# First head group of a hybrid mLSTM/SSD decoder layer: the order of its projection units, and the engine that evacuates the values

## Chip, cores and metric

One core of one Trainium2 chip. The metric is the device time of one execution in microseconds (us), the median of three runs.

## What is computed

The reference is a trunk of two layers (D_MODEL 1024, SEQ 256, everything float32). Each layer runs a SwiGLU feed-forward half step, the mixer, a second feed-forward half step and a gated per-layer input. The change lies in the mixer:

```python
u = rmsnorm(h, g_mix[i])
proj = u @ w_in[i]
q, k, v, o_pre, i_pre, f_pre, z, xbc, dt_raw, gate_pre = jnp.split(proj, split_at, axis=-1)
ha = mlstm_chunkwise(q, k, v, i_pre + b_igate[i], f_pre + b_fgate[i])
ha = rmsnorm(ha, g_mlstm_head[i]) * jax.nn.sigmoid(o_pre)
xbc = jax.nn.silu(causal_dwconv(xbc, conv_w[i], conv_b[i]))
xs, bm, cm = jnp.split(xbc, ...)
dt = jax.nn.softplus(dt_raw + dt_bias[i])
yb = ssd_chunked(xs, dt, -jnp.exp(a_log[i]), bm, cm)
yb = rmsnorm((yb + xs * d_skip[i]) * jax.nn.silu(z), g_ssm_out[i])
merged = sigmoid(g_a) * (ha @ w_branch_a[i]) + sigmoid(g_b) * (yb @ w_branch_b[i])
h = h + merged @ w_out[i]
```

There are four head groups. The 256 tokens are two chunks of 128.

## The kernel before, in words

**Units.** All weights go through in units of 1 MB (8 blocks of 128 rows by 256 columns) in a ring of three slots. For each unit the SyncE queue loads the raw weights (`load`, L285 to L290), ScalarE rounds them to a high part (`hi`, L518), VectorE subtracts to get the low part (`lo`, L823), and TensorE multiplies high by high, high by low and low by high. A feature-major unit (`feat`, L1377) is 48 matmuls over all 256 tokens; the values' unit (`tok`, L1389 to L1391) has the tokens as its output rows, chunk 0 first and then chunk 1. `unit_done` counts finished units, and `hi` of a slot waits for the unit that used the slot before.

**A head group** has nine units, in this order: BC (B and C), QK, X01, X23, V, Z0, Z1, O, GA. Unit number p writes PSUM bank p modulo 3, and VectorE evacuates it (`evac`, L1034; V at L1118; QK at L1104 and L1106). `evac` is one semaphore that counts these evacuations in order. `unit` on TensorE waits for the low part of its weights and for the evacuation that frees its bank.

**Each engine has its order written out by hand** in `groups`, with one body for the first group and one for the other three, which run in a loop. `step(p)` on ScalarE and on VectorE is `hi` and `lo` of unit p + 2. So the order of the steps among the other operations sets when weights are ready.

**The norm ahead of the first group.** `features` (L540, ScalarE) evacuates the transposed activations of a chunk to `u_hi`; `low` (L866, VectorE) makes `u_lo`; `mean_square` (L549) the sums of squares. For the mixer (n == 1) VectorE does both chunks' residuals (L872) first and then both chunks' `low`. Units are not scaled by the norm on their way in; `rms` is applied in the evacuation: `row_scale` makes a diagonal (`rdiag`, L853, VectorE), TensorE spreads it over partitions (`norm_rows`, L1431), ScalarE copies it to `rB` (L569).

**Once per layer, inside the first group:** TensorE multiplies the 40 columns of gates and dt (`small`, L1522); VectorE scales the rows (`pre_row`, L1097); TensorE turns them back (`small_back`, L1528); VectorE computes softplus and `dA` (`softplus_gates`, L950 to L982; the exponential at L653 and `e_a` at L655 are ScalarE's); TensorE transposes (`gates`, L1535 to L1539); VectorE scans the gate rows (`gate_rows`, L989 to L1012), TensorE turns them to columns (`gates_back`, L1545), ScalarE writes `tokc` (L671, L672).

**Per group:** a causal convolution of four taps on three pairs of tiles (`conv`, L1045 and L1048, VectorE), each followed by a tanh on ScalarE (`tanh_conv`, L625) and a product on VectorE (`silu`, L1059). GpSimd builds `R` (L424), from which TensorE makes the decays (`segments`, L1563; `from_start`, L1569) and ScalarE their exponentials (`decay`, L630; L638). GpSimd multiplies them by the masked scores (L464, L468) and the mLSTM weights by a mask (L458). VectorE clips distances (L1075), weighs scores (L1087), masks (L1081) and weights the inputs (L1125, L1129). TensorE does `scores` (L1584), `cb` (L1577), `chunk_heads` (L1592), the transposes of the inputs (L1602), `memory_read` (L1608), `state` (L1614) and `outputs` (L1625, L1627). The head norm (L1169 to L1189) ends in transposes (L1686). In the loop body `from_start` stands in the middle of the V unit, and it waits for `decay(1)`, which ScalarE does behind the tanh of the second convolution.

Of the kernel before, what the change touches and what calls it, by code (L numbers as in the profile page):

```python
# [12 lines left out]
P = 128  # L13
# [10 lines left out]
def trunk(nc, T, out):  # L24
# [36 lines left out]
    BC, QK, X01, X23, V, Z0, Z1, O, GA = range(GU)  # L61
    K_MIX = U_FFN
# [6 lines left out]
    NE = NG * GU + 4  # L69
# [4 lines left out]
    with ctx:  # L74
# [134 lines left out]
        r_i, a5 = at("r_i", [MH, S], F32, a5)  # L209
        r_f, a5 = at("r_f", [MH, S], F32, a5)  # L210
# [35 lines left out]
        names = """up0_done h1T_done res_done uT_done gate_done y_out_ready rB_ready z_tanh o_tanh gate_tanh evac par_ready rdiag_ready rB_done ydiag_ready yB_done yB_ready wsm_hi_ready wsm_ready pre_row_ready pre_ready acs_exp cs_ready y_done ysum_ready  # L246
# [36 lines left out]
        def _(sp):  # L283
# [54 lines left out]
            for lay in range(DEPTH):  # L338
                ffn(0, T["w1_ffn1"], T["w3_ffn1"], T["w2_ffn1"], lay)
                for g in range(0, NG):  # L340
# [12 lines left out]
                    two_cols(BC, g * P + C_B)  # L353
                    two_cols(QK, g * P + C_Q)
                    one(X01, g * (4 * P) + C_X)
                    one(X23, g * (4 * P) + C_X + NP)
                    one(V, g * NP + C_V)
                    one(Z0, g * (4 * P) + C_Z)
                    one(Z1, g * (4 * P) + C_Z + NP)
                    one(O, g * NP + C_O)  # L360
                    one(GA, g * NP + C_G)
# [136 lines left out]
        def _(act):  # L498
# [53 lines left out]
            def norm(lay, n, order, weights):  # L552


                features(lay, n, 0, order)
                if n == 1:
                    features(lay, n, 1, order)
                    weights()
                    mean_square(lay, n, 0)
                else:  # L560
                    weights()
                    mean_square(lay, n, 0)
                    features(lay, n, 1, order)
                mean_square(lay, n, 1)
# [47 lines left out]
            def groups(lay):  # L612
                def body(g, first):
# [6 lines left out]
                    def scaled(p):  # L620
                        act.wait_ge(sem["evac"], lay * NE + g * GU + (p + RING + 1))

# [22 lines left out]
                    step(0)  # L645
                    step(1)
                    if first:
                        row_scale(lay, 1)
                    tanh_conv(0, bcv[:, :, :])
                    if first:  # L650

                        act.wait_ge(sem["x_abs"], lay + 1)
                        a_.activation(sp_b[:, :, :], sp_a[:, :, :], ACT.Exp, scale=-1.0).then_inc(sem["sp_exp"], 1)  # L653
                        act.wait_ge(sem["row_bcast"], 1)
                        a_.activation(e_a[:, :], row_all[:, lay, 40:72], ACT.Exp).then_inc(sem["ea_ready"], 1)  # L655
# [6 lines left out]
                    step(2)  # L662
                    if first:
                        step(3)
# [7 lines left out]
                        a_.activation(tokc[:, 2:6, :], tk[:, 2:6, :], ACT.Exp).then_inc(sem["tok_ready"], 1)  # L672
                        tanh_conv(1, xcv[:, 0:2, :])
                        score_exp()
                        step(5)
                        decay(1)
                        transposed_copies()
                        decay_from_start()
                        tanh_conv(2, xcv[:, 2:4, :])
                    else:  # L680
                        decay(0)
                        step(3)
                        tanh_conv(1, xcv[:, 0:2, :])
                        score_exp()
                        decay(1)
# [3 lines left out]
                        transposed_copies()  # L689
                        step(5)  # L690
                    scaled(Z0)
                    a_.activation(zth[:, :, :], zs[:, 0:2, :], ACT.Tanh, scale=0.5).then_inc(sem["z_tanh"], 1)
                    step(6)
# [31 lines left out]
            for lay in range(DEPTH):  # L725
# [17 lines left out]
                act.wait_ge(sem["wsm_loaded"], lay * 32 + 32)  # L743
                a_.activation(wsm_hi[:, :, :], wsm[:, :, :], ACT.Copy).then_inc(sem["wsm_hi_ready"], 1)
# [4 lines left out]
                for q in range(4):  # L749
# [4 lines left out]
                    act.wait_ge(sem["evac"], lay * NE + (NG * GU + q + RING + 1))  # L754
# [55 lines left out]
        def _(dve):  # L810
# [64 lines left out]
            def residuals(lay, n, stage, last, order, weights):  # L875
# [10 lines left out]
                if n == 1:  # L886
                    joined(1)
                    low(lay, n, 0, order)
                    low(lay, n, 1, order)
                    weights()  # L890
                else:
                    low(lay, n, 0, order)
                    joined(1)
                    weights()
                    low(lay, n, 1, order)

            def row_scale(lay, n):
                variance(lay, n)
                dve.wait_ge(sem["rms_ready"], lay * 4 + n + 1)
                scale_diagonal("rdiag_ready")  # L900
# [85 lines left out]
            def gate_rows(lay):  # L986

                dve.wait_ge(sem["row_tr"], lay + 1)
                ch.add(v_.tensor_copy(r_i[:, :], bank[6][0:MH, 0:S]))  # L989
                ch.add(v_.tensor_copy(r_f[:, :], bank[6][0:MH, S:2 * S]))  # L990
                ch.wait()
                for c in range(NC):
                    s = slice(c * P, (c + 1) * P)
                    ch.add(v_.tensor_tensor_scan(r_b[:, s], ones[0:MH, :], r_f[:, s], 0.0, ALU.mult, ALU.subtract))
# [21 lines left out]
            def groups(lay):  # L1016
# [4 lines left out]
                def body(g, first):  # L1021
# [6 lines left out]
                    def unit_done(p):  # L1028
                        dve.wait_ge(sem["unit_done"], lay * NU + g * GU + (K_MIX + p + RING + 1))
# [799 lines left out]
```

## Time and profile before

| | |
|---|---|
| median of 3 runs | 1619.88 us (1619.72 to 1620.32) |
| the profiled execution | 1620.02 us, its span 1618.3 us |
| TensorE busy | 1580.8 us, 98% of the span |
| VectorE busy | 1047.0 us, 65% |
| ScalarE busy | 731.1 us, 45% |
| GpSimd busy | 215.0 us, 13% |
| chain that ended last | TensorE 86%, VectorE 8%, issue 3%, ScalarE 2% |
| mean DMA rate | 167 GB/s |

The execution's own time is 1.7 us over its span. The first head group of layer 0 runs from about 201 to 283 us, that of layer 1 from about 999 to 1081 us; three more groups of 64 us each follow. "Busy" sums instructions that overlap in the pipeline, and a wait is given to the engine that ended it. Lines are those of the kernel before.

### The profile page before, as it was taken

What the parts mean: (1) busy time and instruction counts of PE and PEld (TensorE: products, weight loads), DVE (VectorE), ACT (ScalarE), POOL (GpSimd) and SP (SyncE); (2) the same over time, 40 slices, a digit from 0 to 9 for tenths busy, and PEclk for the clock granted to TensorE, in tenths of its full rate; (3) what the DMA queues carried; (4) which work ended last, traced back from release to release, by engine and by line L of the source; (5) the groups of instructions that cost most, each with busy time, mean ns of one, the idle gap of its engine ahead of it and who ended that gap; (6) DMA issues with size and microseconds to landing.
All of it is one profiled execution on the core that took longest, in us unless ns stands there. A gap on an engine that the chain in (4) does not pass through costs nothing.

```text
span 1618.3 us, 24373 instructions
## 1 busy us (share of the span) xinstructions
PE 1580.8 (98%) x9778; PEld 1383.6 (86%) x9778; DVE 1047.0 (65%) x1287; ACT 731.1 (45%) x885; POOL 215.0 (13%) x182
## 2 busy tenths in 40 slices
PE   7999989999999999999999999899999999999997
PEld 6888788999999978888888888888999999788886
DVE  5554489788876555454665455888888765554545
ACT  6344343445445345443564445344344533544444
POOL 1000023353330000000000000243344100000000
PEclk9999999999999999999999999999999999999999
DMA  8555534465445645555565555345544465466551
GB/s 257 193 182 183 180 106 132 129 181 140 146 130 182 207 157 194 202 181 183 174 191 184 187 185 147 111 128 154 174 138 130 155 200 187 142 210 196 190 182 65
DMA packets 245077, 270.92 MB, mean 167 GB/s; under 512 B 12560, under 2 KB 226152, under 8 KB 245012
## 3 DMA queue, kind: packets, MB, share of 16 engines
q1 hardware_dynamic: 239504, 266.90, 52.2%
q10 hardware_dynamic: 5364, 2.98, 0.7%
q8 instruction: 44, 0.72, 0.2%
q14 instruction: 21, 0.17, 0.0%
q0 software_dynamic: 144, 0.15, 0.0%
HBM read 268.94 MB, written 1.05 MB: 167 GB/s over the span
## 4 chain that ended last, share of the span: by engine, by line
PE 86%; DVE 8%; issue 3%; ACT 2%; POOL 1%; DMA 1%; SPq 0%; POOLq 0%; ACTq 0%; DVEq 0%
PE bank L1377 27%; PE bank L1403 16%; PE bank L1405 16%; PE bank L1404 16%; DVE xcv L1048 2%; DVE w_lo L823 2%; PE bank L1447 1%; PE bank L1563 1%; PE bank L1766 1%; PE bank L1625 1%; PE bank L1569 1%; DVE xcv L1045 1%; PE bank L1398 1%; DMA w_raw<-in_w_ffn_dram 1%; DVE bcv L1048 1%
## 5 line engine op out<-in xcount | busy, mean ns | idle before, releaser
L823 DVE TENSOR_TENSOR w_lo<-w_raw,w_hi 128x2048 fp32r<-128x2048 f32 x248 | 580.6, 2344 | 287.2 <-ACT w_hi L518 287.2
L518 ACT ACTIVATE w_hi<-w_raw 128x2048 fp32r<-128x2048 f32 x248 | 473.2, 1912 | 214.6 <-PE bank L1405 114.3
L1377 PE MATMUL bank<-u_hi,w_hi 128*128 128x256 f32 x1152 | 335.9, 292 | 2.6 <-DVE u_lo L866 2.6
L1377 PE MATMUL bank<-u_lo,w_hi 128*128 128x256 f32 x1152 | 322.1, 280 | 0.0
L1377 PE MATMUL bank<-u_hi,w_lo 128*128 128x256 f32 x1152 | 321.9, 279 | 0.0
L1403 PE MATMUL bank<-w_hi,ha_hi 128*128 128x512 f32 x704 | 279.4, 397 | 1.8 <-DVE ha_lo L866 0.9
L1405 PE MATMUL bank<-w_hi,ha_lo 128*128 128x512 f32 x704 | 275.4, 391 | 0.0
L1404 PE MATMUL bank<-w_lo,ha_hi 128*128 128x512 f32 x704 | 274.9, 390 | 0.0
L1377 PEld LDWEIGHTS bank<-u_hi,w_hi 128*128 128x128 f32 x1152 | 219.1, 190 | 9.5 <-issue 8.7
L1377 PEld LDWEIGHTS bank<-u_lo,w_hi 128*128 128x128 f32 x1152 | 219.0, 190 | 5.1 <-issue 4.8
L1377 PEld LDWEIGHTS bank<-u_hi,w_lo 128*128 128x128 f32 x1152 | 219.0, 190 | 0.0
L1403 PEld LDWEIGHTS bank<-w_hi,ha_hi 128*128 128x128 f32 x704 | 132.7, 189 | 29.0 <-DVE w_lo L823 1.5
L1405 PEld LDWEIGHTS bank<-w_hi,ha_lo 128*128 128x128 f32 x704 | 132.7, 188 | 28.5
L1404 PEld LDWEIGHTS bank<-w_lo,ha_hi 128*128 128x128 f32 x704 | 132.9, 189 | 26.2
L417 POOL TENSOR_TENSOR rms<-var,m_half 128x2 f32<-128x2 f32 x11 | 7.7, 697 | 1059.4 <-DVE var L859 1046.1
L1403 PE MATMUL bank<-w_hi,h_hi 128*128 128x512 f32 x352 | 138.0, 392 | 0.5
L1405 PE MATMUL bank<-w_hi,h_lo 128*128 128x512 f32 x352 | 137.1, 390 | 0.0
L1404 PE MATMUL bank<-w_lo,h_hi 128*128 128x512 f32 x352 | 137.0, 389 | 0.0
L581 ACT ACTIVATE h_hi<-bank 128x512 fp32r<-128x512 f32 x44 | 26.3, 598 | 160.9 <-PE bank L1447 160.9
L576 ACT ACTIVATE sa<-bank,rms 128x256 f32<-128x256 f32 x88 | 41.7, 474 | 112.7 <-PE bank L1405 103.8
L917 DVE TENSOR_TENSOR h_lo<-bank,h_hi 128x512 fp32r<-128x512 f32 x44 | 30.4, 691 | 92.8 <-ACT h_hi L581 92.8
L1403 PEld LDWEIGHTS bank<-w_hi,h_hi 128*128 128x128 f32 x352 | 66.1, 188 | 15.4 <-issue 2.1
(274 smaller groups left out, 2368.3 us busy)
## 6 DMA issues: line engine op xcount, KB each, us to landing
w_raw<-in_w_ffn_dram SPq DMA_DIRECT2D x262, 512.0 KB, 4.2
w_raw<-in_w_in_dram SPq DMA_DIRECT2D x160, 512.0 KB, 4.9
w_raw<-in_w_branch_b_dram SPq DMA_DIRECT2D x32, 512.0 KB, 4.5
w_raw<-in_w_branch_a_dram SPq DMA_DIRECT2D x16, 512.0 KB, 4.5
w_raw<-in_w_out_dram SPq DMA_DIRECT2D x16, 512.0 KB, 3.9
w_raw<-in_w_ple_gate_dram SPq DMA_DIRECT2D x16, 512.0 KB, 4.6
y_feat<-in_w_ple_dram ACTq DMA_DIRECT2D x2, 1024.0 KB, 4.9
h<-in_x_dram SPq DMA_DIRECT2D x2, 512.0 KB, 5.7
```

What stands on the lines that cost most here:

```text
L518: a_.activation(whi[slot][:, :, :], raw[slot][:, :, :], ACT.Copy).then_inc(sem["w_hi"], 1)
L576: a_.activation(sa[:, c, :], bank[6 - 2 * b + c][:, 0:NP], ACT.Silu, scale=rms[:, c:c + 1]).then_inc(sem["silu_done"], 1)
L581: a_.activation(h1_hi[b][:, :, :], two(6 - 2 * b), ACT.Copy).then_inc(sem["h1_hi_ready"], 1)
L823: v_.tensor_tensor(wlo[slot][:, :, :], raw[slot][:, :, :], whi[slot][:, :, :].bitcast(F32), ALU.subtract).then_inc(sem["w_lo"], 1)
L917: v_.tensor_tensor(h1_lo[b][:, :, :], two(6 - 2 * b), h1_hi[b][:, :, :].bitcast(F32), ALU.subtract).then_inc(sem["h1_ready"], 1)
L1045: ins = v_.tensor_scalar(dst[:, q, :], src, gcw[:, 0, t:t + 1], gcb[:, t:t + 1], ALU.mult, ALU.add)
L1048: ins = v_.scalar_tensor_tensor(out=dst[:, q, :], in0=src, scalar=gcw[:, j, t:t + 1], in1=dst[:, q, :], op0=ALU.mult, op1=ALU.add)
L1377: i = mm(o, w[slot][:, k, cs], x[:, k, :], start=(k + q == 0 and not seeded), stop=(k == KD - 1 and q == 2 and not seeded), skip_group_che ...
L1398: ins = nc.tensor.transpose(bank[b][:, chunk(t)], h[:, c, (4 * q + t) * P:(4 * q + t + 1) * P], ident[:, :])
L1403: mm(o, xh, wh, start=start, stop=False, skip_group_check=True)
L1404: mm(o, xh, wl, start=False, stop=False, skip_group_check=True)
L1405: return mm(o, xl, wh, start=False, stop=stop, skip_group_check=True)
```

## The change

- First group: the order of units is V, BC, QK, X01, X23, Z0, Z1, O, GA. V's matmuls wait for `u_lo` block by block, chunk 0 first, and the transposes of chunk 1 stand in the middle of V's chunk 0.
- The norm of the mixer takes chunk 0 ahead of chunk 1 on ScalarE and VectorE, with a unit's high and low part between them. The rounding of the 40 small columns moves ahead of the last `mean_square`, and `variance` ahead of the group.
- ScalarE evacuates V in every group and signals `v_ready`; V is out of the `evac` count. In the first group ScalarE also makes `rdiag`.
- First group on VectorE: row scale, softplus, then BC, QK and gate rows, then the convolutions. `gate_rows` reads PSUM directly, without two copies.
- First group on TensorE: `small` and `norm_rows` directly behind V, `small_back` in BC, `gates` in X01, `gates_back` and `scores` behind X23, `cb` behind Z0, `chunk_heads` behind Z1, the input transposes behind O, and GA ahead of the last outputs.
- Groups 1 to 3 keep their order except that V's evacuation goes from VectorE (ahead of the third `silu`) to ScalarE (behind the transposed copies).

```diff
+    FIRST = (V, BC, QK, X01, X23, Z0, Z1, O, GA)
+    SCALED = (BC, QK, X01, X23, Z0, Z1, O, GA)
...
             def norm(lay, n, order, weights):
                 features(lay, n, 0, order)
+                weights()
+                mean_square(lay, n, 0)
+                features(lay, n, 1, order)
                 if n == 1:
...
+                    act.wait_ge(sem["wsm_loaded"], lay * 32 + 32)
+                    a_.activation(wsm_hi[:, :, :], wsm[:, :, :], ACT.Copy).then_inc(sem["wsm_hi_ready"], 1)
                 mean_square(lay, n, 1)
...
+                    def values():
+                        p = (FIRST if first else LATER).index(V)
+                        act.wait_ge(sem["unit_done"], lay * NU + g * GU + (K_MIX + p + RING + 1))
+                        for c in range(NC):
+                            i = a_.activation(vtok[:, c, 0:MV], bank[p % RING][:, c * MV:(c + 1) * MV], ACT.Copy,
+                                              scale=rms[:, c:c + 1])
+                        i.then_inc(sem["v_ready"], 1)
...
+                        act.wait_ge(sem["rms_ready"], lay * 4 + 2)
+                        for c in range(NC):
+                            i = a_.activation(rdiag[:, c, :], ident[:, :], ACT.Copy, scale=rms[:, c:c + 1])
+                        i.then_inc(sem["rdiag_ready"], 1)
+                        values()
+                        act.wait_ge(sem["row_bcast"], 1)
+                        a_.activation(e_a[:, :], row_all[:, lay, 40:72], ACT.Exp).then_inc(sem["ea_ready"], 1)
+                        step(0)
+                        row_scale(lay, 1)
+                        step(1)
...
+                        step(5)
+                        decay(1)
+                        tanh_conv(0, bcv[:, :, :])
+                        score_exp()
+                        decay_from_start()
+                        step(6)
+                        tanh_conv(1, xcv[:, 0:2, :])
+                        transposed_copies()
+                        tanh_conv(2, xcv[:, 2:4, :])
...
                 joined(0)
...
+                low(lay, n, 0, order)
+                joined(1)
+                weights()
+                low(lay, n, 1, order)
...
+                        step(0)
+                        dve.wait_ge(sem["rB_ready"], lay + 1)
+                        dve.wait_ge(sem["small_done"], lay + 1)
+                        v_.tensor_tensor(pre_row[:, :], bank[7][0:40, 0:S], rB[0:40, :], ALU.mult)\
+                            .then_inc(sem["pre_row_ready"], 1)
+                        step(1)
+                        softplus_gates(lay)
+                        step(2)
+                        dve.wait_ge(sem["group_ready"], G + 1)
+                        evac(BC, xin[:, 0, :, 3:])
+                        queries_and_keys()
+                        gate_rows(lay)
+                        step(3)
+                        taken(BC)
+                        conv(0, 0, (0, 1), bcv[:, :, :])
+                        evac(X01, xin[:, 1, :, 3:])
+                        silu(0, bcv[:, :, :])
                         distances()
...
                         step(4)
+                        taken(X01)
+                        conv(1, 1, (2, 3), xcv[:, 0:2, :])
                         weigh_scores()
                         mask_cb()
+                        evac(X23, xin[:, 0, :, 3:])
+                        silu(1, xcv[:, 0:2, :])
+                        step(5)
+                        taken(X23)
+                        conv(2, 0, (4, 5), xcv[:, 2:4, :])
+                        dve.wait_ge(sem["ysum_ready"], G + 1)
+                        evac(Z0, zs[:, 0:2, :])
+                        silu(2, xcv[:, 2:4, :])
+                        step(6)
+                        weighted_inputs()
+                        gate_half(0)
+                        evac(Z1, zs[:, 2:4, :])
+                        step(7)
...
+                        unit(V, lambda *a: tok(*a, between=chunk1, ready=(lay * 4 + 1) * 16))
                         small(lay)
...
+                        norm_rows(lay, 1)
+                        unit(BC, lambda *a: feat(*a, between=lambda: small_back(lay)))
+                        unit(QK, feat)
+                        unit(X01, lambda *a: feat(*a, between=lambda: gates(lay)))
                         segments(0, 0)
                         segments(0, 1)
...
+                        unit(X23, feat)
+                        gates_back(lay)
+                        evac(QK)
+                        scores()
```

## Rows read from the trace of the kernel before

**Rows 1.** Waits of TensorE, whole span: waiter, releaser, us in total, times, longest

```profile
PE bank L1535 <- DVE dA L982: 8.1, 2, 4.1
PE bank L1377 <- DVE u_lo L866: 2.6, 2, 1.3
PE bank L1569 <- ACT seg L630: 2.4, 6, 0.5
PE bank L1608 <- ACT cst L695: 1.9, 2, 0.9
PE bank L1686 <- DVE num L1189: 1.7, 2, 0.9
PE bank L1398 <- DVE h L872: 1.6, 2, 0.8
```

**Rows 2.** Stretches of first groups and of group 2: busy us (instructions) by engine, granted clock

```profile
201.60:204.80 3.20, 1.12 (x9) 0.91 (x9) 3.19 (x11) 1.75 (x7) 0.00 (x0) 1.00 0.01 3
...
230.50:234.00 3.50, 3.44 (x18) 3.22 (x19) 3.46 (x6) 0.20 (x1) 3.41 (x2) 0.55 0.08 7
...
1001.80:1005.20 3.40, 3.40 (x18) 3.40 (x19) 2.78 (x8) 3.40 (x8) 0.00 (x0) 0.57 0.02 5
...
347.50:411.50 64.00, 63.63 (x529) 59.01 (x529) 53.08 (x76) 28.64 (x35) 26.50 (x19) 1.00 0.51 147
```

**Rows 3.** Timeline of TensorE: X23's first matmul, the next segment, `cb`, `from_start` of group 1

```profile
231.44 0.56 PE L1377 MATMUL bank<-u_hi,w_hi 128*128 128x256 f32 x1
...
238.31 0.59 PE L1563 MATMUL bank<-xwe,tri_gt 128*128 128x512 f32 x1
...
249.80 0.38 PE L1577 MATMUL bank<-bcv 128*128 128x128 f32 x2
...
313.33 0.70 PE L1569 MATMUL bank<-xwe,ones 128*128 128x512 f32 x1 [0.37 <-ACT seg L630]
```

**Rows 4.** Timeline of ScalarE: high parts and the table load

```profile
209.68 3.75 ACT L518 ACTIVATE w_hi<-w_raw 128x2048 fp32r<-128x2048 f32 x2
...
224.48 1.28 ACT L653 ACT_TABLE_LOAD   x1
```

**Rows 5.** Timeline of VectorE in layer 0

```profile
220.31 0.74 DVE L1045 TENSOR_SCALAR bcv<-xin,gcw,gcb 128x256 f32<-128x256 f32 x2
221.09 2.71 DVE L1048 SCALAR_TENSOR_TENSOR bcv<-xin,gcw,bcv 128x256 f32<-128x256 f32 x6
...
248.28 0.88 DVE L1118 TENSOR_SCALAR vtok<-bank,rms 128x256 f32<-128x256 f32 x2
249.07 2.28 DVE L823 TENSOR_TENSOR w_lo<-w_raw,w_hi 128x2048 fp32r<-128x2048 f32 x1
...
251.94 2.82 DVE L1045 TENSOR_SCALAR xcv<-xin,gcw,gcb 128x256 f32<-128x256 f32 x2
254.79 6.84 DVE L1048 SCALAR_TENSOR_TENSOR xcv<-xin,gcw,xcv 128x256 f32<-128x256 f32 x6
...
262.94 0.68 DVE L1034 TENSOR_TENSOR zs<-bank,rB 128x512 f32<-128x512 f32 x1
...
273.26 0.42 DVE L1169 TENSOR_TENSOR num<-bank,cst 128x257 f32<-128x257 f32 x1
...
325.10 3.92 DVE L823 TENSOR_TENSOR w_lo<-w_raw,w_hi 128x2048 fp32r<-128x2048 f32 x1
```

**Rows 6.** Timeline of GpSimd: products of decays and scores, groups 0 and 1

```profile
252.10 4.87 POOL L464 TENSOR_TENSOR seg<-seg,cbm 128x1024 f32<-128x1024 f32 x2 [3.10 <-DVE cbm L1081]
...
326.83 4.46 POOL L468 TENSOR_TENSOR cs<-cs,bcv 128x1024 f32<-128x1024 f32 x1
```

**Rows 7.** Chain of waits, pieces: start us, us, engine, line, instructions

```profile
267.12 5.66 PE bank L1377 x48
...
1036.83 1.72 PE bank L1563 x4
1041.27 1.43 PE bank L1545 x12
```

More of the change, by code:

```diff
@@ L351, in one @@
                         load(K_MIX + g * GU + p, s, *dcols(W, lay, c, s), lay)
[L353 to L361, printed above, removed]
+                    columns = {BC: g * P + C_B, QK: g * P + C_Q, X01: g * (4 * P) + C_X, X23: g * (4 * P) + C_X + NP,
+                               V: g * NP + C_V, Z0: g * (4 * P) + C_Z, Z1: g * (4 * P) + C_Z + NP,
+                               O: g * NP + C_O, GA: g * NP + C_G}
+                    for p, u in enumerate(LATER if g else FIRST):
+                        (two_cols if u in (BC, QK) else one)(p, columns[u])
                 for i in range(4):
@@ L689, in body @@
                         transposed_copies()
+                        values()
                         step(5)
@@ L1107, in body, with queries_and_keys @@
-                    silu(0, bcv[:, :, :])
-                    if first:
-                        softplus_gates(lay)
-                        step(2)
-                        gate_rows(lay)
-                    else:
-                        step(2)
-                        distances()
-                    def values():
-                        unit_done(V)
-                        for c in range(NC):
-                            i = v_.tensor_scalar(vtok[:, c, 0:MV], bank[1][:, c * MV:(c + 1) * MV], rms[:, c:c + 1],
-                                                 None, ALU.mult)
-                        i.then_inc(sem["evac"], 1)
+                    def queries_and_keys():
+                        unit_done(QK)
+                        b = place_of(QK) % RING
+                        v_.scalar_tensor_tensor(out=qT[:, :], in0=bank[b][:, 0:S], scalar=MQK ** -0.5, in1=rB[:, :],
+                                                op0=ALU.mult, op1=ALU.mult)
+                        v_.tensor_tensor(kT[:, :], bank[b][:, S:2 * S], rB[:, :], ALU.mult).then_inc(sem["evac"], 1)
@@ L1144, in body @@
                         step(4)
+                        taken(X01)
+                        conv(1, 1, (2, 3), xcv[:, 0:2, :])
                         weigh_scores()
                         mask_cb()
-                    taken(X23)
-                    conv(2, 0, (4, 5), xcv[:, 2:4, :])
-                    if not first:
-                        values()
-                    silu(2, xcv[:, 2:4, :])
-                    if not first:
+                        evac(X23, xin[:, 0, :, 3:])
+                        silu(1, xcv[:, 0:2, :])
@@ L1379, in feat, with tok @@
                 i.then_inc(sem["unit_done"], 1)
-            def tok(slot, b, xh, xl, between=None):
+            def tok(slot, b, xh, xl, between=None, ready=None):
                 for c in range(NC):
-                    if c and between:
+                    if c and between and ready is None:
                         between()
@@ L1388, in tok @@
                     for k in range(KD):
+                        if ready is not None:
+                            if c == 0 and k == KD // 2:
+                                between()
+                            pe.wait_ge(sem["u_lo_ready"], ready + c * KD + k + 1)
                         mm(o, xh[:, k, cs], whi[slot][:, k, :], start=(k == 0), stop=False)
@@ L1688, in body @@
                     i.then_inc(sem["hnT_done"], 1)
-                    unit(GA, feat)
+                    if not first:
+                        unit(GA, feat)
                 body(0, True)
```

224 lines of the change are left out of this document (92 added, 132 removed).

## The prediction

> **What bounds the kernel now.** I read the engine shares first: TensorE is busy 98% of the span. Then its waits. They come to about 16 us: 8.1 for `dA`, 2.6 for `u_lo`, 1.6 for the residual, 1.9 and 1.7 late in the first groups, all in the first group of a layer, and 2.4 for decays at `from_start` in groups 1 to 3 [rows 1]. Then the granted clock: in layer 0 the stretch behind the wait for `dA` ran at 0.55, so mostly at 1.2 instead of 2.4 GHz, and in layer 1 the first unit at 0.57; in layer 0 the clock stayed at 1.00 there although the waits ahead of it were the same [rows 2]. Because of that X23 took 6.87 us from its first matmul to the next instruction [rows 3] where a unit takes 5.66 [rows 7].
>
> Last I asked which wait ends last. A later group takes 64.0 us and TensorE works 63.6 of them [rows 2]. The remaining 0.4 is `from_start`, which waits for ScalarE's `decay(1)` [rows 3]. That hangs behind VectorE's convolutions, and these, back through the evacuations, behind the group before. So a later group hangs on the hand-over between VectorE and TensorE, and what the first group saves is kept only as far as **VectorE** arrives earlier in group 1. TensorE alone being early buys nothing. That decides this change.
>
> **Until V and BC.** V needs only chunk 0 for its first half. TensorE goes from the feed-forward into V without the waits of 0.8 and 1.3 [rows 1], stops for some 0.3 and 0.2 (the second residual stands behind eight `low`s; chunk 1's `low`s behind a low part) and ends V near 208.4. `small` follows, 2.8, then `norm_rows`, and three quarters of BC: 215.9.
>
> **ScalarE's new queue.** `rms` is there at about 208.7. Behind it stand `rdiag` (0.55, two narrow copies), the values (0.7; 0.88 on VectorE, which loses both), the table load, 1.28 [rows 4], `e_a` with its start 0.3, and only then the high part of QK, 1.87 (3.75 for two [rows 4]): 213.5. VectorE idles some 5.7 us for it, then needs a low part (2.28, of which 0.08 overlaps [rows 5]) and `pre_row` 0.4: 216.1. TensorE waits 0.3 for it instead of 4.0 for `dA`, which is now ready by 224 while `gates` comes at 228. The saved 4 us keep the clock up there as well.
>
> The load's price carries this queue. The Trainium skill, page "ScalarE: Activation LUTs", section on the table-load gate, puts such a load at about 2.7 us including the drain. By that VectorE and everything behind it would be 1.4 later per layer and the whole sum 2.2 to 2.8 worse; the trace shows 1.28 and I take that.
>
> **TensorE to the decays.** From 216.15: the last quarter of BC 1.4, QK, X01 and X23 at 5.66 to 5.76 each [rows 7], four segments 3.4 and `gates_back` 1.43 [rows 7], and `small_back`, `gates` and `scores`, some 2.3 as an estimate from `gates_back`'s 12 matmuls. That is 25.7: 241.9, where the same segments ended at 249.8 [rows 3]. TensorE is 8 us ahead.
>
> **What gives it back.** VectorE reaches the end of its first convolution at about 240. But on ScalarE `tanh_conv(0)` now stands behind `decay(1)`, so the tanh ends near 243.2 and VectorE idles about 2.5. From 243.3 to the addition at L1169 it has to do: four low parts 8.8, two convolutions 6.9 (0.74 and 2.71 each [rows 5]), six evacuations and products of 512 columns 3.7 (0.68 less overlap [rows 5]), distances, weighing and mask 1.25, weighted inputs 1.95, gate half 0.6: 23.2. To that come GpSimd's products. Before, the last convolution took 2.82 and 6.84 instead of 3.45 beside them, 6.2 more [rows 5, 6]; in group 1 a low part took 3.92 and GpSimd's own product 4.46 beside it [rows 5, 6]. They exclude each other. In the new order they meet `silu(1)`, a low part and the start of the convolution: 1.8 + 2.2 + 2.2 = 6.2 again, plus 0.65 for the mask product and 0.25 for a tanh. 243.3 + 23.2 + 7.1 = 273.6. Before it was 273.26 [rows 5].
>
> So the 8 us are gone by the end of the group. The same bookkeeping over the order of before ends 0.8 to 1.0 late, mostly because it charges the exclusion too high; so VectorE arrives between 0.3 later and 1.0 earlier. I take **0.65 earlier** in layer 0. The two copies that leave `gate_rows` (0.8) lie under the idle 2.5 and count nothing; scans that read PSUM may cost up to 0.5, hidden by the same idle time. Layer 1 ran 0.9 longer than layer 0 over the same code, because of its slow first unit; without that, 0.65 + 0.9 = **1.55**. SyncE's loads keep 8 us between a low part and the next high part of the slot and stay hidden.
>
> **The new wait.** TensorE enters group 1 about 6 us ahead of VectorE's clock. It waits some 1.4 for X01's low part, 1.1 for QK's evacuation, and at `from_start`, where it comes at 309.4 and the decays come at 313.1, **3.6**. Waits of 4.0 and 4.1 took the clock down both times before [rows 1, 2]. Here V's second half and Z0 follow, and VectorE waits for Z0: this slow stretch is on the path. Its price lies between 0 and 1.8 (X23 plus `gates` in layer 1); I take X23's 6.87 − 5.66 = **1.2** per layer, the nearest row.
>
> **Groups 1 to 3.** VectorE loses the values, 0.88 [rows 5]; mask and Z1's low part come 0.8 earlier, GpSimd's products finish earlier, and the low part behind them is blocked for less than its 1.7. ScalarE has room for 0.7. The gain can't exceed what TensorE waits, 0.4 a group, since with that gone TensorE is the bound: 0 to 2.4 in both layers. I take 0.3 for two groups per layer, 1.2; the first of the three hangs on group 0.
>
> **Sum:** −0.65 − 1.55 + 2 × 1.2 − 1.2 = −1.0, on the profiled execution's 1620.02 (1.7 of it outside the span; 0.14 over the median). Forecast 1618.9. That is within 0.2% (3.2 us), about what a measurement of this kernel can tell from no change.
>
> **Rivals.**
> - *The clock holds* through the 3.6 us wait. For it: layer 0's first unit stayed at full clock behind 2.1 us of waits. Against: both waits of 4 us. Time: 1618.9 − 2.4 = 1616.5. Chance 0.15; it lies at the edge of 0.2%, half on either side.
> - *GpSimd's products fall beside evacuations.* If the ports are given in another order, one of three products per layer costs VectorE nothing, 2.2 each, and the wait at `from_start` shrinks to 1.4, so that the clock holds: 1618.9 − 4.4 − 2.4 = 1612.1; half of it 1615.5. For it: an evacuation does stand among them, at X23. Against: behind it everything up to Z0's evacuation reads SBUF twice. Chance 0.2. The Trainium skill, page "SBUF — State Buffer", section "Who interferes with whom", says that a VectorE instruction with at most one SBUF input does not contend, and that the one that issues first blocks the other; by that rule this order is possible but not forced.
> - *TensorE is kept*: the waits of rows 1 vanish (15 us) and group 1 does not give them back, 1620 − 13 = 1607. That needs VectorE 8 us earlier. Chance 0.05.
> - *Slower: the clock falls inside group 0 too.* Late in the group TensorE stops for O's and GA's low parts and for `silu(2)`, 2.0 + 1.3 + 0.9 in 10 us. In layer 1 waits of 0.8 and 1.3 were enough. A slow GA, `state` and outputs cost 1.2 to 1.8 each layer, and `state` has only 0.1 to spare before it delays the head norm; with 1.8 at both places and no gain in groups 1 to 3, 1620.02 − 2.2 + 3.6 + 3.6 = 1625.0, with 1.2 at each place and the gain kept 1621.4. It decides once the granted clock of that stretch is below 1. Chance 0.13.
> - *It doesn't do what it says*: with ScalarE's queue late by another 2 us (the loads, the table), TensorE would stop at `small_back` and the sum would be about zero, 1620 to 1622. Chance 0.05, within 0.2%.
>
> The forecast itself (1617.5 to 1620.5) has 0.42. Faster by over 0.2%: 0.05 + 0.2 + 0.07 = 0.32. Slower by over 0.2%: 0.09. Within: 0.59. The range, leaving out the 1607 and the far end of the slow case, is 1613.0 to 1622.5.
>
> **What would show it.** Right: no wait for `dA`; TensorE 7 us earlier at the start of group 1's BC (277.7); then waits at L1377 for `w_lo`, at `scores`, and about 3.6 at `from_start` for `seg`, with a clock near 0.55 behind it; VectorE idle 5 to 6 ahead of QK's low part and 2 to 3 ahead of `silu(0)`; L1169's addition within 1 us of 273.3. Wrong: L1169 several us earlier, or group 1 without the wait at `from_start`; or groups 2 and 3 no longer 64.0.

## The result, and the profile after

The changed kernel takes **1611.32 us** (median of 5 runs, 1610.51 to 1612.93) against 1619.88 us for the kernel before on the same chip (5 runs, 1619.72 to 1622.06): a ratio of 0.9945, 95% interval 0.9931 to 0.9960. The forecast was 1618.9, its range 1613.0 to 1622.5. The kernel is 8.6 us faster, and the time lies below the range. The profiled execution took 1611.34 us with a span of 1609.6.

First the page's engine shares of the kernel after, then the waits of TensorE over the whole span (waiter, releaser, us in total, times, longest), which answer to [rows 1].

```profile
PE 1576.6 (98%) x9778; PEld 1378.2 (86%) x9778; DVE 1043.3 (65%) x1263; ACT 737.4 (46%) x905; POOL 223.0 (14%) x182
```

```profile
PE bank L1389 <- DVE w_lo L834: 6.0, 6, 1.6
PE bank L1712 <- DVE num L1202: 2.7, 2, 1.4
PE bank L1627 <- DVE xcv L1059: 2.1, 2, 1.1
...
PE bank L1617 <- ACT vtok L623: 1.4, 2, 0.7
PE bank L1609 <- DVE kT L1095: 1.3, 2, 0.7
```

The waits for `dA`, `u_lo`, the residual, `cst` and `from_start` are gone. Instead there are six waits for a low part and a few small ones, about 13.5 us in all against 18 before, none of them in groups 2 and 3, where `from_start` had waited 0.4 us in each before. TensorE's busy time fell by 4.2 us with the same 9778 matmuls, which I put down to the clock: in the windows of the kernel after (us from the start, busy us (instructions) by engine, granted clock, DMA share, GB/s), nothing of the mixer is slow any more, where [rows 2] had 0.55 and 0.57.

```profile
226.00:240.00 14.00, 14.00 (x103) 12.29 (x103) 12.30 (x23) 4.95 (x7) 3.70 (x5) 1.00 0.43 120
1018.00:1032.00 14.00, 14.00 (x110) 12.81 (x109) 12.34 (x22) 4.24 (x8) 4.82 (x5) 1.00 0.35 96
307.00:321.00 14.00, 13.31 (x99) 11.96 (x99) 11.36 (x22) 7.53 (x12) 4.06 (x2) 1.00 0.28 95
```

TensorE's timeline of the kernel after: X23's first matmul (230.46), the next segments, `from_start`, `cb`, the wait of O, BC of group 1 (276.61), and group 1's X01, `scores`, `from_start` and `chunk_heads`; it answers to [rows 3].

```profile
230.46 0.68 PE L1389 MATMUL bank<-u_hi,w_hi 128*128 128x256 f32 x1
...
239.01 1.02 PE L1588 MATMUL bank<-xwe,tri_gt 128*128 128x512 f32 x2
...
244.97 1.02 PE L1594 MATMUL bank<-xwe,ones 128*128 128x512 f32 x2
...
248.07 0.60 PE L1602 MATMUL bank<-bcv 128*128 128x128 f32 x4
...
257.43 0.38 PE L1389 MATMUL bank<-u_hi,w_hi 128*128 128x256 f32 x1 [1.58 <-DVE w_lo L834]
...
276.61 0.37 PE L1389 MATMUL bank<-u_hi,w_hi 128*128 128x256 f32 x1
...
290.29 0.38 PE L1389 MATMUL bank<-u_hi,w_hi 128*128 128x256 f32 x1 [0.76 <-DVE w_lo L834]
...
298.44 0.71 PE L1609 MATMUL bank<-qT,kT 128*128 128x128 f32 x4 [0.66 <-DVE kT L1095]
...
307.62 1.02 PE L1594 MATMUL bank<-xwe,ones 128*128 128x512 f32 x2
...
319.23 0.67 PE L1617 MATMUL bank<-vtok,ktok 128*128 128x257 f32 x2 [0.69 <-ACT vtok L623]
```

The row that decides is 307.62: group 1's `from_start` waits for nothing. ScalarE's timeline of the kernel after says why: the table load and QK's high part, then the first group's tanh, then group 1's `decay(1)` (302.86), which now stands ahead of the tanh of the second convolution (309.45), and the values.

```profile
209.57 1.28 ACT L662 ACT_TABLE_LOAD   x1
...
211.00 1.90 ACT L517 ACTIVATE w_hi<-w_raw 128x2048 fp32r<-128x2048 f32 x1
...
241.42 0.62 ACT L629 ACTIVATE cth<-bcv 128x512 f32<-128x512 f32 x1
...
302.86 1.08 ACT L634 ACTIVATE seg<-bank 128x512 f32<-128x512 f32 x2
...
309.45 0.63 ACT L629 ACTIVATE cth<-xcv 128x512 f32<-128x512 f32 x1 [5.51 <-DVE xcv L1048]
...
318.24 0.84 ACT L623 ACTIVATE vtok<-bank,rms 128x256 f32<-128x256 f32 x2
```

I had overlooked that hunk of the diff. **The description of the change ahead of the prediction is incomplete**: it says that groups 1 to 3 keep their order but for V's evacuation, and its diff leaves this out:

```diff
                         step(3)
+                        decay(1)
                         tanh_conv(1, xcv[:, 0:2, :])
                         score_exp()
-                        decay(1)
                         step(4)
```

VectorE's timeline of the kernel after, layer 0 (answers to [rows 5]), and GpSimd's products beside it ([rows 6]):

```profile
212.94 2.29 DVE L834 TENSOR_TENSOR w_lo<-w_raw,w_hi 128x2048 fp32r<-128x2048 f32 x1 [5.58 <-ACT w_hi L517]
...
242.08 0.69 DVE L1059 SCALAR_TENSOR_TENSOR bcv<-cth,bcv 128x512 f32<-128x512 f32 x1 [1.74 <-ACT cth L629]
...
250.79 2.20 DVE L1059 SCALAR_TENSOR_TENSOR xcv<-cth,xcv 128x512 f32<-128x512 f32 x1 [0.23 <-ACT cth L629]
252.91 4.46 DVE L834 TENSOR_TENSOR w_lo<-w_raw,w_hi 128x2048 fp32r<-128x2048 f32 x1
257.30 2.81 DVE L1045 TENSOR_SCALAR xcv<-xin,gcw,gcb 128x256 f32<-128x256 f32 x2
...
271.69 0.42 DVE L1182 TENSOR_TENSOR num<-bank,cst 128x257 f32<-128x257 f32 x1
```

```profile
250.04 5.19 POOL L463 TENSOR_TENSOR seg<-seg,cbm 128x1024 f32<-128x1024 f32 x2 [3.97 <-DVE cbm L1081]
255.19 4.44 POOL L467 TENSOR_TENSOR cs<-cs,bcv 128x1024 f32<-128x1024 f32 x1
```

**Where the time went.** What lies outside the two mixers differs between the profiled executions, whatever the kernel: it took 1051.1 to 1052.9 us in most of them, 1050.6 in e6 and 1054.0 in e1. So I measured the mixer alone, from its first transpose (197.77 before, 197.42 after, in layer 0) to the matmul with `ysum` behind group 3, and split it at the first group's addition at `num`. All from the timelines; "rest" is the tail of group 0 and groups 1 to 3. Each pair is layer 0 / layer 1, from one profiled execution of each kernel.

| kernel | start to `num` of group 0 | rest | mixer | gained, both layers |
|---|---|---|---|---|
| before | 75.49 / 76.82 | 208.05 / 207.70 | 283.54 / 284.52 | |
| after | 74.27 / 74.27 | 205.66 / 205.46 | 279.93 / 279.73 | 8.4 |
| e1 new first group, loop as before | 74.27 / 74.51 | 207.30 / 207.48 | 281.57 / 281.99 | 4.5 |
| e2 first group as before, new loop | 75.51 / 76.24 | 205.49 / 205.69 | 281.00 / 281.93 | 5.1 |
| e3 after, `decay(1)` late | 74.27 / 74.53 | 208.85 / 209.02 | 283.12 / 283.55 | 1.4 |
| e4 after, V on VectorE in the loop | 74.26 / 74.25 | 205.47 / 205.58 | 279.73 / 279.83 | 8.5 |
| e5 before, `decay(1)` early | 76.49 / 76.16 | 205.95 / 206.08 | 282.44 / 282.24 | 3.4 |
| e6 after, one tanh ahead | 73.66 / 73.65 | 205.63 / 205.58 | 279.29 / 279.23 | 9.5 |

The first groups gave 1.22 + 2.55 = 3.8 us, the rest 2.39 + 2.24 = 4.6. How far such numbers repeat can be seen in e12 below, the kernel after once more: 74.51 / 74.24 to `num`, 205.58 / 205.60 for the rest. The old first group repeats less well: before, e2 and e5 share it, and it took 75.5 to 76.8 us. The mixers' 8.4 are nearly all of the profiled executions' 1620.02 − 1611.34 = 8.7.

### The profile page after: what moved, and what is told of

Same layout as the page of the kernel before. It is cut to its first block, busy times and chain, and to the rows that moved or that the text cites. A ratio compares the mean times of both kernels' runs of the same rounds, so it can differ in the third digit from the quotient of the medians.

```text
span 1609.6 us, 24365 instructions
## 1 busy us (share of the span) xinstructions
PE 1576.6 (98%) x9778; PEld 1378.2 (86%) x9778; DVE 1043.3 (65%) x1263; ACT 737.4 (46%) x905; POOL 223.0 (14%) x182
## 4 chain that ended last, share of the span: by engine, by line
PE 85%; DVE 7%; issue 3%; ACT 2%; POOL 1%; DMA 1%; SPq 0%; DVEq 0%; ACTq 0%; POOLq 0%
PE bank L1389 27%; PE bank L1419 16%; PE bank L1420 16%; PE bank L1421 16%; DVE w_lo L834 2%; PE bank L1588 1%; PE bank L1463 1%; ACT w_hi L517 1%; DVE xcv L1048 1%; PE bank L1793 1%; PE bank L1414 1%; PE bank L1650 1%; PE bank L1594 1%; PE bank L1405 1%; DVE zs L1099 1%
```

## The experiments

Edits are against the kernel named in each heading; where no other is named, ratios are to the kernel before on the same chip, with 95% intervals.

**e1 and e2: the two halves of the change.** e1 is the kernel after with the loop body of groups 1 to 3 as before, e2 the kernel before with the loop body of after:

```diff
 # e1, loop body
-                        decay(1)
                         tanh_conv(1, xcv[:, 0:2, :])
                         score_exp()
+                        decay(1)
                         step(4)
...
-                        values()
```

In e1 VectorE evacuates V again ahead of the third `silu`; e2 is the reverse of both on the kernel before.

> The changed kernel with the loop body of groups 1 to 3 as it was before: decay(1) back behind the exponential of the scores, V evacuated by VectorE. Theory A (the first group only brings TensorE early; the loop's earlier decay(1) is what lets it keep that): about 1617 to 1620 us, with a wait of 3 to 4 us at from_start in group 1 of each layer and a lower granted clock behind it. Theory B (the first group's order brings the gain by itself): 1611 to 1613 us.

> The kernel before with the loop body of the changed one: decay(1) ahead of the second tanh, V evacuated by ScalarE in groups 1 to 3. Theory A: TensorE only loses its six waits of 0.4 us at from_start, so 1617.5 to 1619.9 us, since the first group is as late as ever; the two parts are worth much more together than the sum of each alone. Theory B: 1619.5 to 1620.5 us, nothing. A third theory, C (the loop is what was gained): 1612 to 1614 us.

e1: 1617.54 us, 0.9985 (0.9976 to 0.9994). e2: 1616.21 us, 0.9974 (0.9965 to 0.9983). Each half gives something alone, 4.5 and 5.1 us of mixer time, where both together give 8.4; but 0.6 of e2's lies in its first groups, in which nothing was changed. By the medians the halves give 3.1 and 4.4 us and the whole change 8.6. So I see no large bonus in having both, and one of about 1 us is not excluded. By the table "rest" is 4.6 us shorter with the new loop and the old first group, just as with the whole change. So groups 1 to 3 could give more than the 0.4 us each that I had allowed. In e1 the wait that I had forecast is there, in both layers. TensorE's timeline of e1:

```profile
313.21 1.13 PE L1598 MATMUL bank<-xwe,ones 128*128 128x512 f32 x2 [3.16 <-ACT seg L634]
...
1108.50 1.13 PE L1598 MATMUL bank<-xwe,ones 128*128 128x512 f32 x2 [2.84 <-ACT seg L634]
```

**e3: the overlooked line alone.** The kernel after with only `decay(1)` back behind `score_exp()` in the loop.

> The changed kernel with decay(1) alone moved back behind the exponential of the scores in the loop. Theory A: within 1 us of the kernel with the whole old loop, 1617 to 1619 us, a wait of 3 to 4 us at from_start in group 1. Theory B: 1611 to 1613 us.

1619.92 us, 0.9997 (0.9988 to 1.0006). This is the kernel that my prediction describes, since only V's engine is changed in its loop: forecast 1.0 us faster than the kernel before, measured 0.7 (1620.61 on the same chip). With one line of a loop put back, nothing is left of the 8.6 us that the time could tell from no change; the mixers keep 1.4. That it comes so close is in part luck: the first groups gave 3.5 us where I forecast 2.2, and "rest" cost 2.1 where I forecast 1.2. The wait is that of e1, and behind it the clock goes down. TensorE's timeline and the windows of e3, then the same two windows of e1 with a third, in its first group of layer 1:

```profile
312.22 1.13 PE L1594 MATMUL bank<-xwe,ones 128*128 128x512 f32 x2 [3.15 <-ACT seg L634]
...
1108.96 2.08 PE L1594 MATMUL bank<-xwe,ones 128*128 128x512 f32 x2 [2.84 <-ACT seg L634]
```

```profile
310.00:324.00 14.00, 11.78 (x76) 10.55 (x77) 9.12 (x16) 8.39 (x13) 5.03 (x2) 0.88 0.19 60
1102.00:1116.00 14.00, 11.16 (x70) 9.00 (x70) 11.10 (x22) 5.43 (x8) 0.93 (x1) 0.88 0.46 147
```

```profile
310.00:324.00 14.00, 10.84 (x82) 9.83 (x82) 10.70 (x20) 7.65 (x11) 4.77 (x2) 1.00 0.26 80
1102.00:1116.00 14.00, 11.16 (x86) 10.00 (x85) 12.40 (x26) 5.94 (x11) 1.47 (x2) 1.00 0.45 142
1046.00:1060.00 14.00, 12.10 (x87) 11.59 (x85) 13.77 (x15) 2.52 (x4) 9.57 (x3) 0.88 0.43 112
```

0.88 over 14 us is 1.7 us of clock, and e3's "rest" is 1.55 and 1.54 longer than e1's (208.85 − 207.30, 209.02 − 207.48).

**e4: V's evacuation alone.** The kernel after with V back on VectorE in groups 1 to 3.

> The changed kernel with V's evacuation alone given back to VectorE in groups 1 to 3. Theory A: VectorE has 0.8 us more to do in a group in which it is the one that is waited for (group 1), and the wait of 0.7 us at chunk_heads goes: 1611.3 to 1613.0 us. Rival: ScalarE's evacuation is what counts in the loop, 1615 us or more.

1612.25 us, 0.9953 (0.9939 to 0.9966), and a mixer of 279.73 / 279.83, that of after. Moving V to ScalarE in the loop is worth nothing that shows in this kernel. It takes 0.88 us from VectorE, but in group 1 TensorE then waits 0.7 for `vtok`, where in e4 it waits 0.4 for the weighted inputs.

**e5: the decay's place alone, on the kernel before.**

```diff
                         step(3)
+                        decay(1)
                         tanh_conv(1, xcv[:, 0:2, :])
                         score_exp()
-                        decay(1)
                         step(4)
```

> The kernel before with one edit: in groups 1 to 3 ScalarE does decay(1) ahead of the tanh of the second convolution. Theory (the decay's place in the loop is what freed the later groups; V's engine is worth nothing): about the time of the version with both loop edits, 1616 to 1617 against about 1620.5, no wait at from_start in any group, 0.6 us less per later group. Rival (V on ScalarE carries half of that gain): 1618 to 1619, groups of about 63.6 us.

1616.50 us (9 runs, 1615.21 to 1617.13), 0.9974 (0.9964 to 0.9984): the time of e2 with one line moved. From one head norm's transposes to the next the last two groups of layer 0 take 63.30 us each, where they took 63.94 and 64.04. The recorded wait at `from_start` was 0.37 of these 0.64 (and 0.38 of 0.74). TensorE's timelines around group 2's `from_start` show where the rest lies, first in the kernel before, then in e5:

```profile
376.72 0.28 PE L1391 MATMUL bank<-w_hi,u_lo 128*128 128x256 f32 x1
377.37 1.12 PE L1569 MATMUL bank<-xwe,ones 128*128 128x512 f32 x2 [0.37 <-ACT seg L630]
378.33 1.02 PE L1569 MATMUL bank<-zth,ones 128*128 128x512 f32 x2
```

```profile
376.55 0.28 PE L1391 MATMUL bank<-w_hi,u_lo 128*128 128x256 f32 x1
376.67 1.02 PE L1569 MATMUL bank<-xwe,ones 128*128 128x512 f32 x2
377.52 1.02 PE L1569 MATMUL bank<-zth,ones 128*128 128x512 f32 x2
```

Without the wait, `from_start` starts 0.12 us after the start of V's last matmul, overlapping it; with the wait, 0.65 after. That is 0.53 and not 0.37, since the record counts idle time only from the end of the matmul in front. Another 0.11 is the first matmul behind the wait, which overlaps with nothing (0.96 from `xwe` to `zth`, against 0.85).

Of e2's 4.6 us in "rest", e5 gives 3.7 (2.10 + 1.62 in the table). What e2 has more lies in group 1, which from transposes to transposes takes 63.30 in e2 and 63.87 in e5, in both layers. No wait stands behind these 0.57: the matmuls of e5's first 16 us there each start a little later than e2's. The kernel after has the same 63.87 in group 3 of layer 1 and 63.30 in that of layer 0, with V on ScalarE in both. So it is no effect of V's engine, and its cause stays open.

**e6: the idle time ahead of `silu(0)`.** The kernel after, first group:

```diff
                         step(5)
+                        tanh_conv(0, bcv[:, :, :])
                         decay(1)
-                        tanh_conv(0, bcv[:, :, :])
                         score_exp()
```

> The kernel after with one edit in the first group: ScalarE does the tanh of the first convolution ahead of decay(1), so that VectorE's idle time of 1.7 us ahead of silu(0) shrinks to about 0.6. Theory A (VectorE's clock sets the end of the first group): all of VectorE is 1.1 us earlier from there on, the waits for O's low part (1.6) and X01's in group 1 (0.8) shrink, mixer 0.8 to 1.2 us shorter per layer, 1609 to 1610. Theory B (GpSimd's products and the later hand-overs take it back): the addition at num less than 0.4 us earlier and no difference in time.

1610.23 us, 0.9941 (0.9928 to 0.9955). `num` comes 0.6 us earlier in each layer and most of it reaches the end of the mixer (279.29 / 279.23 against 279.93 / 279.73). That is half way between my two theories. VectorE's idle time ahead of `silu(0)` fell by 1.34 us, to 0.40, but behind it a wait of 0.63 for the matmuls of `cb` is new, and the one for the next tanh grew from 0.23 to 0.84. So `silu(1)` began at the same distance from the mixer's start as in the kernel after (53.36 and 53.37 us). What came 0.6 us earlier is the mask `cbm`, with it GpSimd's product, and with the product's end the end of `silu(1)`, which took 1.59 instead of 2.20.

**e7: the table load later.** The kernel after with `e_a`, and so the load, behind `step(1)`.

> The kernel after with one edit in the first group: e_a, and with it the load of the exponential's table (1.28 us), goes behind the high parts of QK and X01. Theory A (VectorE is caught again by its wait for the transposed gates, so this queue has slack): QK's low part 1.3 us earlier, the scans no earlier, addition at num within 0.2 us, same time as after. Theory B (my prediction's: what is late in this queue is late for all of VectorE): 1.3 us gained per layer, 1609.

1611.10 us, 0.9945 (0.9931 to 0.9958). VectorE's idle time ahead of QK's low part falls from 5.58 to 4.03, by 1.55, as large as load and `e_a` together; the wait ahead of the scans grows from 1.42 to 3.20; `num` 74.40, mixer 279.85 / 279.80. Making the queue that I costed with most care shorter gains nothing, and theory B fell: VectorE is caught again by the transposed gates. The Trainium skill (page "ScalarE: Activation LUTs", section on the table-load gate) gives about 2.7 us for such a load together with a drain. The trace shows 1.28 for the load, and `e_a`, the next instruction, starts at 210.87, 0.02 behind its end; no drain shows. What a longer load would cost no run tests. It would not simply have vanished in the wait ahead of the scans: TensorE comes to the transposes of `pre_row` at 215.61, just as VectorE frees them (215.56), so it would have been delayed as well, and the transposed gates with it.

**e8: V ahead of the tanh.** The kernel after, loop: `values()` ahead of `tanh_conv(2)`.

> The kernel after with one edit in groups 1 to 3: ScalarE evacuates V ahead of the tanh of the third convolution instead of behind the transposed copies. Theory A (TensorE is the bound in group 1, so its wait of 0.7 us at chunk_heads counts in full): that wait goes, 0.7 us per layer, 1610 against 1611.3. Theory B (VectorE's clock sets group 1): the wait moves to a low part or to the head norm's transposes and the time stays; the tanh is not delayed since ScalarE idles 2.9 us ahead of it.

1613.15 us (1611.87 to 1614.85), 0.9957 (0.9943 to 0.9971), mixer 279.91 / 279.80, so the 2 us that its median lies over e7's do not come from the mixer. The wait at `chunk_heads` is gone and another has come, that of `state` for VectorE's weighted inputs. This is theory B. TensorE's timeline of e8:

```profile
328.82 1.13 PE L1639 MATMUL bank<-xwe,btok 128*128 128x512 f32 x2 [0.44 <-DVE xwe L1110]
```

**e9: the two copies of the gate rows back.**

```diff
+                ch.add(v_.tensor_copy(r_i[:, :], bank[6][0:MH, 0:S]))
+                ch.add(v_.tensor_copy(r_f[:, :], bank[6][0:MH, S:2 * S]))
+                ch.wait()
```

> The kernel after with the two copies of the gate rows back and the scans reading SBUF, as in the kernel before. Theory A (my prediction's: they lie under VectorE's idle time ahead of silu(0), 1.7 us, and ahead of the scans): VectorE's first convolution begins some 1.5 us later, the idle time shrinks to about 0.3, the addition at num within 0.3 us of after, no difference in time. Theory B (VectorE is behind all the way and they were a real saving): num 1.5 us later, 3 us slower, 1614.

1611.79 us, 0.9944 (0.9931 to 0.9958), mixer 280.37 / 279.79. The idle time ahead of `silu(0)` shrank from 1.74 to 0.95, and `num` came 0.25 later in one layer (74.52), no later in the other (74.24). The kernel after, run again as e12, has the same two numbers within 0.01, so the copies cost nothing that shows. This is theory A. VectorE's timeline of e9:

```profile
228.91 0.40 DVE L991 COPY r_f<-bank 4x256 f32<-4x256 f32 x1
229.34 0.73 DVE L995 TENSOR_TENSOR_SCAN r_b<-ones,r_f 4x128 f32<-4x128 f32 x2
```

The two scans take 0.73 from SBUF here and 0.72 from PSUM in the kernel after. Reading PSUM costs nothing here; the 1.60 that they took in the kernel before, from 233.40, lay beside a GpSimd instruction that ran from 233.58 to 234.72.

**e10: what bounds the first group now.** The kernel after with GpSimd's products in the first group cut from eight heads to one; the other seven heads' products of decays and scores, and those of `cs`, are left out, so this kernel computes something else and serves only as a measurement.

```diff
+                nh = 1 if first else EH
...
-                    g_.tensor_tensor(seg[:, c, :, :], seg[:, c, :, :],
-                                     cbm[:, c, :].unsqueeze(1).broadcast_to([P, EH, P]), ALU.mult)\
+                    g_.tensor_tensor(seg[:, c, 0:nh, :], seg[:, c, 0:nh, :],
+                                     cbm[:, c, :].unsqueeze(1).broadcast_to([P, nh, P]), ALU.mult)\
...
```

> The kernel after with GpSimd's three products in the first group of each layer cut to one head of eight (the other heads' products are left out of the computation). It measures what bounds the first group now. Theory A (VectorE's clock, which these products block for about 5.8 us per layer): silu(1), the low part and the convolution behind it go back to 0.7, 2.3 and 0.74 us, the addition at num comes 4 to 5 us earlier, TensorE's waits for O's and GA's low parts, silu(2) and the head norm's transposes (4.4 us per layer) shrink to under 1, mixer 3.5 to 5 us shorter per layer: 1602 to 1605. Theory B (TensorE itself or ScalarE's hand-overs bound it): under 1.5 us per layer, 1608.5 or more.

1603.15 us, 0.9890 (0.9875 to 0.9905), 8.2 under the kernel after and 8.6 under e9, which ran on the same chip. In layer 0 `num` is at 70.26 and the mixer 275.78, 4.0 and 4.15 us less. VectorE's timeline of e10, to be held beside 250.79, 252.91 and 257.30 above:

```profile
251.37 0.78 DVE L1060 SCALAR_TENSOR_TENSOR xcv<-cth,xcv 128x512 f32<-128x512 f32 x1
252.07 2.55 DVE L835 TENSOR_TENSOR w_lo<-w_raw,w_hi 128x2048 fp32r<-128x2048 f32 x1
254.55 0.73 DVE L1046 TENSOR_SCALAR xcv<-xin,gcw,gcb 128x256 f32<-128x256 f32 x2
```

The three groups of instructions are 1.4 + 1.9 + 2.1 = 5.4 us shorter, and 4 of them reach the end. TensorE's waits for O's and GA's low parts and for `silu(2)` are gone; that of the head norm stays at 1.3, where I had expected it to go as well. This is theory A: VectorE's clock (how far it has got in its work, not its frequency), and in it GpSimd's exclusion, bounds the first group.

**e11 and e12: a better version, beside the kernel after.** e11 is e6 with, in the first group, also `tanh_conv(1)` ahead of `step(6)`; e12 is the kernel after unchanged.

> The kernel after with two edits on ScalarE in the first group: the tanh of the first convolution ahead of decay(1), as in e6, and the tanh of the second ahead of the high part behind it. Theory A (VectorE's clock sets the first group): silu(1) another 0.8 us earlier in its queue, and with GpSimd's product beginning at the same time as before some 0.3 to 0.8 us of that kept at num; mixer 278.4 to 279.0 us against 279.3 in e6 and 279.9 in after, time 1 to 3 us under the kernel after. Theory B (the product only blocks VectorE for as much longer): as e6, mixer 279.3.

> The kernel after, unchanged, on the same chip and in the same rounds as e11, so that the two can be compared: 1611.3 and a mixer of 279.8 us, with a spread of about 1 us between executions that comes from the feed-forward halves.

e11: 1609.83 us (1609.50 to 1611.65), 0.9938 (0.9924 to 0.9951). e12: 1610.98 us (1610.77 to 1611.89), 0.9943 (0.9930 to 0.9957). Mixers 279.30 / 279.35 and 280.10 / 279.83: e11 is 0.5 to 0.8 us a layer shorter than the kernel after and no better than e6. This is theory B: `silu(1)` starts earlier and is blocked for longer, since GpSimd's product ends no earlier. VectorE's timeline of e6, then of e11:

```profile
251.19 1.59 DVE L1059 SCALAR_TENSOR_TENSOR xcv<-cth,xcv 128x512 f32<-128x512 f32 x1 [0.84 <-ACT cth L629]
```

```profile
250.06 2.53 DVE L1059 SCALAR_TENSOR_TENSOR xcv<-cth,xcv 128x512 f32<-128x512 f32 x1
```

Both end at 252.6 to 252.8. e6's version is the best that I found; its lead over the kernel after shows in the mixer's times, not in the intervals.

## Why the prediction was wrong

**The step that failed** is "The new wait", and with it a sentence of "What bounds the kernel now": that a later group hangs on the hand-over between VectorE and TensorE. I read it from the wait for `decay(1)`, "behind VectorE's convolutions", and took this order as fixed. The diff removes it. With `decay(1)` ahead of the tanh, the decays are there at 303.9 and TensorE comes at 307.6, so the 3.6 us and the clock's 1.2 per layer never came due. My own condition named it ("or group 1 without the wait at `from_start`"). e3 puts the line back and is 0.7 us faster than the kernel before, where I forecast 1.0, in part by luck (see e3).

**The waits and the clock, as a term** (+2.4 for both layers): in e3, where they exist, "rest" is 3.2 to 3.6 us a layer longer than in the kernel after. The wait was 3.15 and 2.84 (forecast 3.6), the clock 1.55 (forecast 1.2, with X23 as the nearest row). Both were sized about right, for a kernel that was not this one. That the wait itself costs nothing against the kernel before, and only the clock does, held too: e1 has the wait with the clock at 1.00, and its "rest" is 0.75 and 0.22 us shorter than before.

**Groups 1 to 3** (−1.2, bound 2.4): the bound was wrong. I took the recorded wait of 0.4 as all that a group could give. e5's groups give 0.64 to 0.74, since the record leaves out the overlap of matmuls that the wait prevents. Of the whole gain in "rest", 4.6, e5's one line alone gives 3.7. The values, to which I gave the 1.2, gave nothing that shows (e4).

**The first group** (−0.65 and −1.55): −1.22 and −2.55. The direction and the path were right and the size was little more than half. Step by step against the kernel after: end of V 208.4, measured 208.0; QK's low part 213.5, measured 212.94; `pre_row`'s transposes free at 216.1, measured 215.6; segments done at 241.9, measured 240.9; start of group 1's BC 277.7, measured 276.61; waits in group 1 for X01's low part 1.4 and QK's evacuation 1.1, measured 0.76 and 0.66. VectorE's idle time ahead of `silu(0)` was 1.74 and not 2.5. GpSimd's exclusion is 1.5 + 2.2 + 2.1 = 5.8 us against 6.2, at the three places that I named. (On the timeline `num` moved by 1.57, from 273.26 to 271.69; 0.35 of that is a mixer that starts earlier.) In layer 1 the slow clock had cost more than the 0.9 that I took: the kernel before was 1.33 longer there, the kernel after not at all. This part of the gain hangs on what the clock did in one execution: in e2 and e5, which have the same first group, layer 1 was 0.73 longer and 0.33 shorter than layer 0.

**What gives it back** was right as a mechanism. TensorE led by 8.9 us at the end of the segments (240.9 against 249.8), and e10 shows that the products that block VectorE take 4 us of such a lead per layer. That the copies count nothing held (e9). That the table load carries the queue fell: earlier by its whole length, it gains nothing (e7).

**Rivals.** "GpSimd's products fall beside evacuations" came nearest in time (1612.1), but for a reason that the rows exclude: all three products block VectorE, the last one even an instruction that reads a single tensor from SBUF, the first of the two that take 2.81 us at 257.30 where e10 has 0.73. The rule that I quoted from the Trainium skill (page "SBUF — State Buffer", section "Who interferes with whom") has an exception there for VectorE's 2-port modes, and names `tensor_scalar` and `copy` for them; the row agrees with the exception, which I had left out, though no row shows in which mode the instruction ran. "The clock holds" was true and was only half of it, since the wait went too. "Slower" had its mechanism once, in e1, whose window from 1046 to 1060 us has a clock of 0.88. No cost of it shows: `num` came at 74.51 there, and at 74.53 in e3 and 74.51 in e12 with the clock at 1.00.

The prediction's sum, then: −2.2 forecast against −3.8, and +1.2 against −4.6, with 0.3 more outside the mixer, makes the 7.7 us between −1.0 and −8.7.

## What to carry to other kernels

Before costing a wait that a change seems to lead into, look up in the diff every operation on the path of that wait, in loop bodies too, and not only where the change has its name. A short wait that recurs in every turn of a loop costs more than its record, 0.64 to 0.74 us for 0.37 here, and moving one line that releases it was worth as much as the rearrangement of a whole group. A lead of the bounding engine is kept only as far as the engine that feeds it follows, and that is best measured by removing what blocks the feeder (e10), which also says how much a real fix could bring at most.

## What the runs showed of the hardware

- **The same wait with and without a fall of the clock.** In e1 and e3 TensorE waited 3.16 / 2.84 and 3.15 / 2.84 us at the same place. The granted clock stayed at 1.00 in e1 and went to 0.88 over 14 us in e3 (part of them at 1.2 instead of 2.4 GHz), in both layers. In the loop the two kernels differ only in the engine that evacuates V. Why the clock fell in one and not in the other stays open.
- **Scans** of 4 x 128 take the same from PSUM (0.72 us for two, kernel after) and from SBUF (0.73, e9); from SBUF beside a GpSimd instruction two took 1.60 (kernel before).
- **To start a blocked instruction earlier gains nothing.** Counted from the mixer's start (197.48 in e11, 197.83 in e6), `silu(1)` began 0.8 us earlier in e11 than in e6 and ended 0.2 us later; GpSimd's product began 0.15 us later in e11 (52.15 against 52.00).
- **A recorded wait understates its cost.** The idle time of 0.37 us at `from_start` made group 2 of layer 0 0.64 us longer (before against e5).
